# Conv FFNs on the unnormalised residual: inverse norm at the eviction, tap products from SBUF, norm weight inside the high/low split

## What is computed

```
def rms_norm_2(x, g):
    xf = x.astype(jnp.float32)
    y = xf * lax.rsqrt(jnp.mean(xf * xf, axis=-1, keepdims=True) + NORM_EPS)
    return (y * g.astype(jnp.float32)).astype(x.dtype)

def causal_dwconv(h, w, b):
    c = h.shape[-1]
    y = lax.conv_general_dilated(h, w[:, None, :].astype(h.dtype), (1,), [(CONV_WIDTH - 1, 0)],
                                 dimension_numbers=('NWC', 'WIO', 'NWC'), feature_group_count=c)
    return y + b

def conv_ffn(h, w_up, conv_w, conv_b, w_down):
    u = causal_dwconv(h @ w_up, conv_w, conv_b)
    gate, up = jnp.split(u, 2, axis=-1)
    return (jax.nn.silu(gate) * up) @ w_down
```

## Time and profile before

| | us |
|---|---|
| median of 3 runs | 1832.31 |
| lowest, highest | 1828.08, 1835.67 |
| span of the profiled execution | 1831.9 |
| conv_0, up phase (first to last matmul) | 1267.4 to 1397.0 |
| conv_1, up phase | 1624.8 to 1753.2 |
| PE busy in the span | 1700.7 (93%) |
| DVE busy | 1185.9 (65%) |
| ACT busy | 904.3 (49%) |

### The profile page before, as it was taken

How to read it: one execution, slowest core, us unless ns; L and a number is a source line. 1 busy time by engine, 2 the same in 40 slices (tenths; PEclk the granted TensorE clock), 3 DMA queues, 4 the chain that set the end, 5 groups by cost and what they waited for, 6 DMA issues and landing times.

```text
span 1831.9 us, 33959 instructions
## 1 busy us (share of the span) xinstructions
PE 1700.7 (93%) x13128; PEld 1636.6 (89%) x13128; DVE 1185.9 (65%) x1907; ACT 904.3 (49%) x1546; POOL 14.2 (1%) x20
## 2 busy tenths in 40 slices
PE   6999999899999999996899999878999989779997
PEld 5999997799999999975799999767999988679997
DVE  6555656576666666667666665767886576578764
ACT  5544453454445444454454454355665442356652
POOL 1000000000000000000000000000000000000000
PEclk9999999899999999998899999988999999989999
DMA  7554552255446554540255456204554543035442
GB/s 270 177 182 144 205 199 104 70 202 184 174 155 217 184 183 142 204 153 35 81 197 182 160 166 236 92 15 166 183 184 140 197 190 108 34 137 182 169 158 86
DMA packets 47358, 286.11 MB, mean 156 GB/s; under 512 B 5996, under 2 KB 6764, under 8 KB 23968
## 3 DMA queue, kind: packets, MB, share of 16 engines
q1 hardware_dynamic: 44640, 278.94, 43.5%
q10 hardware_dynamic: 2240, 5.19, 0.8%
q0 software_dynamic: 384, 0.68, 0.1%
HBM read 283.74 MB, written 1.05 MB: 155 GB/s over the span
## 4 chain that ended last, share of the span: by engine, by line
PE 84%; DVE 9%; ACT 4%; issue 2%; DMA 0%; ACTq 0%; DVEq 0%
PE ps_gemm L129 78%; DVE s_wlo L89 3%; ACT s_whi L80 1%; ACT s_work L839 1%; PE ps_gemm L828 1%; PE ps_sum L178 1%; PE ps_gemm L803 1%; DVE s_small L879 1%; DVE s_work L875 1%; PE ps_s L803 1%; PE ps_sum L828 1%; ACT s_work L848 1%; PE ps_sum L760 0%; DVE s_work L898 0%; PE ps_gemm L1161 0%
## 5 line engine op out<-in xcount | busy, mean ns | idle before, releaser
L89 DVE TENSOR_TENSOR s_wlo<-s_wraw,s_whi 128x1024 fp32r<-128x1024 f32 (+3 forms) x608 | 629.5, 1077 | 491.6 <-ACT s_whi L80 491.5
L80 ACT ACTIVATE s_whi<-s_wraw 128x1024 fp32r<-128x1024 f32 (+3 forms) x608 | 539.7, 935 | 445.3 <-PE ps_gemm L129 438.3
L129 PE MATMUL ps_gemm<-s_xhi,s_whi 128*128 128x256 f32 x2504 | 717.2, 286 | 13.4 <-DVE s_xlo L239 9.0
L129 PE MATMUL ps_gemm<-s_xlo,s_whi 128*128 128x256 f32 x2504 | 711.7, 284 | 0.0
L129 PE MATMUL ps_gemm<-s_xhi,s_wlo 128*128 128x256 f32 x2504 | 711.6, 284 | 0.0
L129 PEld LDWEIGHTS ps_gemm<-s_xhi,s_whi 128*128 128x128 f32 x2504 | 483.9, 193 | 18.1 <-issue 11.3
L129 PEld LDWEIGHTS ps_gemm<-s_xlo,s_whi 128*128 128x128 f32 x2504 | 484.0, 193 | 1.3 <-issue 1.0
L129 PEld LDWEIGHTS ps_gemm<-s_xhi,s_wlo 128*128 128x128 f32 x2504 | 483.9, 193 | 0.0
L129 PE MATMUL ps_gemm<-hid_hi,s_whi 128*128 128x256 f32 x1344 | 381.4, 284 | 12.4 <-DVE s_wlo L89 6.9
L129 PE MATMUL ps_gemm<-hid_hi,s_wlo 128*128 128x256 f32 x1344 | 381.3, 284 | 0.0
L129 PE MATMUL ps_gemm<-hid_lo,s_whi 128*128 128x256 f32 x1344 | 380.9, 283 | 0.0
(11 more groups left out here) (322 smaller groups left out, 1248.8 us busy)
## 6 DMA issues: line engine op xcount, KB each, us to landing
s_wraw<-in_stream_dram SPq DMA_DIRECT2D x178, 1024.0 KB, 4.8
s_wraw<-in_stream_dram SPq DMA_DIRECT2D x96, 704.0 KB, 4.1
s_wraw<-in_stream_dram SPq DMA_DIRECT2D x16, 768.0 KB, 4.3
s_wraw<-in_stream_dram SPq DMA_DIRECT2D x14, 512.0 KB, 3.3
...
```

The source lines that it names most:

```text
L80: c.act.activation(c.whi[:, slot, s], c.wraw[:, raw, s], ACT.Copy).then_inc(c.hi_ready, 1)
L89: last = c.dve.tensor_tensor(c.wlo[:, slot, s], c.wraw[:, raw, s], c.whi[:, slot, s].bitcast(F32), ALU.subtract)
L129: last = pe.matmul(out, a, b, start=start and i == 0, stop=stop and i == 2, skip_group_check=skip)
```

## The change

`conv_0` and `conv_1` join `LATE_SCALED`. The mixer's `post_norm` now makes the split ahead for them, and the sums of squares stand between the products of their first unit. In the up iteration VectorE scales the bank by the inverse norm into a new SBUF tile `c.scaled`, which frees the bank. ScalarE's tap 2 reads `c.scaled` and waits for it through `bank_free`; the four products read it too. The rest of the split of tile j-1 moves ahead of the products, and a new semaphore `linear_ready` tells the end of the last product.

In all stages that are scaled late, the separate multiplication by the norm weight goes (it stays for mix_a, which needs `c.xn2`): ScalarE's rounding carries the weight as its scale, and VectorE's subtraction becomes `x * weight - high` in one instruction.

```
-LATE_SCALED = ("mix_a", "ffn2_0", "ffn1_1", "mix_b", "ffn2_1", "mix_e", "mix_o")
+LATE_SCALED = ("mix_a", "ffn2_0", "ffn1_1", "mix_b", "ffn2_1", "mix_e", "conv_0", "mix_o", "conv_1")
+KEPT_SCALED = ("mix_a",)
...
-    c.act.wait_ge(c.xn_ready, cnt.xn + n + 1 + step)
-    c.act.activation(c.xhi2[:, s], c.xn2[:, s], ACT.Copy).then_inc(c.xhi_ready, 1)
+    c.act.activation(c.xhi2[:, s], c.x2[:, s], ACT.Identity, scale=ahead.column(c, n, turn)).then_inc(c.xhi_ready, 1)
...
+    g = ahead.column(c, n, turn)
+    if ahead.kept:
+        c.dve.tensor_scalar(c.xn2[:, s], c.x2[:, s], g, None, ALU.mult).then_inc(c.xn_ready, 1)
     c.dve.wait_ge(c.xhi_ready, cnt.xn + n + 1 + step)
-    c.dve.tensor_tensor(c.xlo2[:, s], c.xn2[:, s], c.xhi2[:, s].bitcast(F32), ALU.subtract).then_inc(c.xlo_ready, 1)
+    c.dve.scalar_tensor_tensor(c.xlo2[:, s], c.x2[:, s], g, c.xhi2[:, s].bitcast(F32), ALU.mult,
+                               ALU.subtract).then_inc(c.xlo_ready, 1)
...
-            last = first_products_pe(c, cnt, bank, u, (c.xlo_ready, cnt.xn + 1), late)
+            last = first_products_pe(c, cnt, bank, u, (c.xlo_ready, cnt.xn + 1), late, name.startswith("conv"))
...
-        if not late:
-            act.wait_ge(c.unit_done, u0 + j + 1 + step)
-            if NF * cnt.two + j >= 2:
-                act.wait_ge(c.hid_ready, NF * cnt.two + j - 1 + step)
-        for side in range(0 if late else 2):
-            act.activation(c.cv[:, j % 2, side, :], c.ps_gemm[:, (g0 + j) % 4, side * T:(side + 1) * T], ACT.Identity,
+        if conv is not None:
+            act.wait_ge(c.bank_free, g0 + j + 1 + step)
+            act.wait_ge(c.hid_ready, NF * cnt.two + j - 1 + step)
+        for side in range(0 if conv is None else 2):
+            act.activation(c.cv[:, j % 2, side, :], c.scaled[:, j % 2, side, :], ACT.Identity,
...
+        dve.wait_ge(c.unit_done, u0 + j + 1 + step)
+        dve.tensor_tensor((c.cv if conv is None else c.scaled)[:, j % 2, :, :], bank.rearrange("p (a b) -> p a b", b=T),
+                          c.inv[:, :].unsqueeze(1).to_broadcast([P, 2, T]), ALU.mult).then_inc(c.bank_free, 1)
+        if j:
+            rest(j - 1, turn)
+        if conv is None:
+            dve.wait_ge(c.bank_free, g0 + j + 1 + step)
+            return
+        dve.wait_ge(c.tap_ready, 2 * m + 2 + step * 2)
+        for back in (1, 2):
             for side in range(2):
                 v = c.cv[:, j % 2, side, back:T]
                 if back == 2:
                     dve.wait_ge(c.back_done, 2 * m + side + 1 + step * 2)
-                ins = dve.scalar_tensor_tensor(v, bank[:, side * T:(side + 1) * T - back],
+                ins = dve.scalar_tensor_tensor(v, c.scaled[:, j % 2, side, 0:T - back],
                                                tap(c, conv, j, side, 2 - back, turn), v, ALU.mult, ALU.add)
-                ins.then_inc(c.back_done if back == 1 else c.conv_ready if side == 0 else c.bank_free, 1)
-        if j:
-            rest(j - 1, turn)
-        dve.wait_ge(c.bank_free, g0 + j + 1 + step)
+                ins.then_inc(c.back_done if back == 1 else c.conv_ready if side == 0 else c.linear_ready, 1)
+        dve.wait_ge(c.linear_ready, m + 1 + step)
```

More of the change, by code:

```diff
@@ L274, in ffn_pe @@
     late = name in LATE_SCALED
-    if name != "ffn1_0" and not late:
-        for k in range(KD):
-            norm_sums_pe(c, cnt, k)
     def up(j, turn):
@@ L366, in silu @@
     def silu(j, step):
-        if late:
+        if conv is None:
             act.wait_ge(c.bank_free, g0 + j + 1 + step)
@@ L412, in ffn_act @@
         cnt.two += 1
-        cnt.conv += not late
+        cnt.conv += conv is not None
     logs_act(c)
@@ L428, in output @@
                        after[:, bass.ds(turn * (2 * T) + n * T, T)], ACT.Square).then_inc(c.sq_ready, 1)
-        if ahead:
-            ahead_hi_act(c, cnt, n, turn, step)
+        if ahead is not None:
+            ahead_hi_act(c, ahead, n, turn)
     with act.Fori(0, KD // 2 - 1) as lap:
@@ L444, in ffn_act, with ffn_dve @@
         split_below(split_hi, c, cnt, u0 + 2 * KD + 2)
-def ffn_dve(c, cnt, name, conv, src, gain, ahead):
+def ffn_dve(c, cnt, name, conv, ahead):
     dve, u0, g0 = c.dve, FIRST_UNIT[name], cnt.out
     late = name in LATE_SCALED
-    if not late and name != "ffn1_0":
-        normed_dve(c, cnt, src, gain)
     split_below(split_lo, c, cnt, u0 + 2)
@@ L485, in convolved @@
         bank = c.ps_gemm[:, (g0 + j) % 4, :]
-        if late:
-            dve.wait_ge(c.unit_done, u0 + j + 1 + step)
-            dve.tensor_tensor(c.cv[:, j % 2, :, :], bank.rearrange("p (a b) -> p a b", b=T),
-                              c.inv[:, :].unsqueeze(1).to_broadcast([P, 2, T]), ALU.mult).then_inc(c.bank_free, 1)
-        else:
-            dve.wait_ge(c.tap_ready, 2 * m + 2 + step * 2)
-        for back in () if late else (1, 2):
+        dve.wait_ge(c.unit_done, u0 + j + 1 + step)
[3 more added lines that the diff above has]
+            rest(j - 1, turn)
+        if conv is None:
+            dve.wait_ge(c.bank_free, g0 + j + 1 + step)
+            return
+        dve.wait_ge(c.tap_ready, 2 * m + 2 + step * 2)
+        for back in (1, 2):
             for side in range(2):
@@ L537, in output @@
         ins.then_inc(c.bank_free, 1)
-        if ahead is not None:
-            dve.wait_ge(c.bank_free, g0 + n + 1 + step)
-            ahead_dve(c, ahead, n, turn)
         add_squares(c, cnt, n, n == 0 and turn is None, step)
         if ahead is not None:
-            ahead_lo_dve(c, cnt, n, turn, step)
+            ahead_lo_dve(c, cnt, ahead, n, turn, step)
     output(0, None)
@@ L572, in add_squares, with all_squares_act @@
     ins.then_inc(c.sq_added, 1)
-def all_squares_act(c, cnt, src, written, value, step=1, ahead=False):
+def all_squares_act(c, cnt, src, written, value, step=1, ahead=None):
     for k in range(KD):
@@ L581, in all_squares_act @@
         c.act.activation(c.sq[:, k % 2, :], src[:, k, :], ACT.Square).then_inc(c.sq_ready, 1)
-        if ahead:
-            ahead_hi_act(c, cnt, k, None, 0)
+        if ahead is not None:
+            ahead_hi_act(c, ahead, k, None)
     cnt.sq += KD
-    if ahead:
+    if ahead is not None:
         cnt.xn += KD
@@ L605, in post_norm_dve @@
             c.dve.tensor_tensor(c.x[:, k - 1, :], c.x[:, k - 1, :], c.xn[:, k - 1, :], ALU.add).then_inc(c.post_added, 1)
[L606 to L608 removed]
         if ahead is not None and 1 < k <= KD + 1:
[L610 removed]
+            ahead_lo_dve(c, cnt, ahead, k - 2, None, 0)
     if ahead is not None:
@@ L615, in post_norm_dve, with post_norm_act @@
     cnt.sq += KD
[L618 removed]
+def post_norm_act(c, cnt, ahead=None):
     inverse_act(c, cnt)
@@ L1072, in project_dve @@
         for k in range(n, n + wide):
-            if ahead is not None:
-                c.dve.wait_ge(c.bank_free, cnt.out)
-                ahead_dve(c, ahead, k, None)
             add_squares(c, cnt, k, k == 0, 0)
             if ahead is not None:
-                ahead_lo_dve(c, cnt, k, None, 0)
+                ahead_lo_dve(c, cnt, ahead, k, None, 0)
     if not post:
@@ L2308, in build @@
         c.gate, c.hid = (c.work[:, i * 2 * T:(i + 1) * 2 * T].rearrange("p (a b) -> p a b", b=T) for i in range(2))
-        c.cv = c.work[:, 4 * T:8 * T].rearrange("p (s a b) -> p s a b", s=2, b=T)
+        c.cv, c.scaled = (c.work[:, i * T:(i + 4) * T].rearrange("p (s a b) -> p s a b", s=2, b=T) for i in (4, 8))
         c.ss, c.pt = c.work[:, 0:3 * 1024].rearrange("p (a b) -> p a b", b=1024), c.work[:, 3 * 1024:4 * 1024]
```

48 lines of the change are left out of this document (22 added, 26 removed).

## The result

Before: 1833.99 us, median of 4 runs (1828.08 to 1837.52). Changed: 1892.61 us, median of 4 (1885.97 to 1894.08). The ratio is 1.0315, with a 95% interval of 1.0292 to 1.0337. I had forecast 1872 and a range up to 1884: the sign and the mechanism were right, the sum and the range were too short. The medians lie 58.6 us apart; the profiled executions have spans of 1892.2 and 1831.9, 60.3 us apart, where my sum had 39.5.

What follows compares the result with a forecast made beforehand. TensorE was taken to bound the kernel, with VectorE's longer cycle overtaking it in the conv up phases. Conv stages +14.2 and +14.8, handovers +12.2, mix_o -1.7 made +39.5 on 1831.9: 1871.4, forecast 1872 us, range 1853 to 1884.

Steps and rivals of the forecast that it cites:

- VectorE's cycle in the counted loop: Conv up phase: one looped VectorE iteration takes 7.01 us against TensorE's 5.76, costing about 21 us per conv stage.
- the rest of down is as before: Conv down phase from unit 24 on: no change in time.
- the 1.7 us that mix_o was to win: Boundary conv_0 to mix_o: dropping the separate norm-weight multiplication (L260) shortens it by 1.7 us.
- the handovers: Up to down in each conv stage: 15.8 us from the up phase's end to unit 24 against 9.7, +6.1 twice.
- The stall: Conv up phase: VectorE stands still 1.6 us per cycle through ScalarE's two taps and one rounding, lifting its cycle above TensorE's.
- S4: Start of VectorE's low half in iteration 4, at 41.4 us from the first post-norm multiplication, after three straight cycles.
- S19: Start of VectorE's low half in iteration 19, at 146.6 us from the first post-norm multiplication, after fifteen looped cycles.
- Taps and products from SBUF: Conv up phase: two taps take 1.05 us, 0.05 over now; products gain nothing from SBUF, within 0.02 us each.
- The boundary: Into the conv stages: sums of squares between the first unit's products win 7.1 us in conv_0 and 6.5 in conv_1.
- S0: Start of VectorE's low half in iteration 0, at 15.35 us from the first post-norm multiplication.
- the shorter chain: Rival in the up phase: shorter looped handoffs and taps give a 6.5 us cycle, 1852 us in all; chance 12%.
- the clock falls: Rival: TensorE, idle 1.2 us in every 7, drops to 1.2 GHz; 2034 us at most; chance 4%.

Runs made afterwards that it cites:

- e1: Changed kernel with ScalarE rounding tile j-1 ahead of the two taps of tile j instead of behind them; 1864.85 us, ratio 1.0168.
- e4: Changed kernel with taps and products reading PSUM, conv inputs not normalised; scaling still done into a tile nobody reads; 1831.39 us, ratio 0.9997.
- e6: Changed kernel with the counted loops of ScalarE's and VectorE's conv up phase written out; 1876.31 us, ratio 1.0248.
- e11: e3 with matmuls nobody reads in TensorE's pauses, fewer than e8 at the boundaries, plus 6 ahead of unit 24; 1818.36 us, ratio 0.9933.
- e9: Kernel before the change with only the norm weight folded into the split; conv stages as they were; 1832.78 us, ratio 1.0005.
- e2: Changed kernel with VectorE's rest of tile j-1 moved back behind the four tap products of tile j; 1867.44 us, ratio 1.0195.
- e10: e3 with the scaling of each conv tile done a second time, into a tile nobody reads; 1840.16 us, ratio 1.0044.
- e5: Like e9 on the kernel before, but by a slip without the weight multiplication in VectorE's low part of the activations; 1831.69 us, ratio 1.0000.
- e3: Changed kernel's same operations, reordered on VectorE and ScalarE so taps and rounding lie beside VectorE's low half; 1827.40 us, ratio 0.9980.
- e8: e3 with matmuls nobody reads in TensorE's boundary pauses, 10 before the last norm's sum and 24 behind it; 1826.55 us, ratio 0.9974.

## Why the prediction was right in its mechanism and short in its sum

The step that failed is the size of VectorE's cycle in the counted loop: 7.01 us in my sum, 7.28 measured in the mean, 8.0 us in both stages together. My range had room for that, as it reached to a cycle of 7.3. What carried the time 8.6 us beyond its end are terms without such room: "the rest of down is as before", where the clock fell (3.5 us), the 1.7 us that mix_o was to win (2.2), the handovers (1.0), and the spread of the stages ahead of conv_0 (3.7), which I had at nothing.

**The stall (right).** The chain of my cycle is in the trace link by link: low half to gate 2.28 (as said), gate to scaling 0.34 (0.33), scaling 0.68 (0.68), handoff 0.18 (0.14), two taps 1.10 (1.05), rounding less its overlap, and handoff, 0.47 (0.48), rest to products 0.34 (0.33), products 1.66 (1.64), completion 0.12 (0.08): 7.17 against 7.01. The straight cycle is 6.81 against 6.75; my own terms, with 0.04 for both handoffs, give 6.80, so I had added that up wrongly. e1 to e4 show that it is the chain.

**The cycle in the loop (the mis-sized term, 8.0 us).** I had left out the end of a lap. One cycle in four is 7.61 and the one behind it 7.27, so a lap has a mean of 7.31, not 7.01. From S4 to S19, fifteen cycles with three turns, it is 109.2 and 109.1 us, 7.28 each, where I had 105.2. Some 0.16 us of the 0.27 missing are in every cycle, the rest at the turns. I had read the loop's cost as a longer handoff (0.14 for 0.04) from a kernel whose loops are covered by TensorE, and there neither the lap's end nor the rest of it can be seen. e6 measured the loop whole: 16 us in the kernel.

**Taps and products from SBUF (right).** Products 479 ns against 474 from PSUM, so no gain. A tap takes 597 ns against 551 from PSUM, 46 more; I had 50. The Trainium skill, "VectorE: DVE Perf Modes", section on the TRN2 errata, has the two engines in one table: for VectorE a smaller fixed cost from SBUF, which these rows again don't show, for ScalarE 224 against 172 cycles, 43 ns at its 1.2 GHz, with which the 46 ns agree.

**The boundary (right in mechanism, 2.3 us short in both together).** The first product of conv_0 comes 6.3 us behind the mixer's last, where I had said about 6. But behind the multiplication it stands at 2.7 us in conv_0 and 3.1 in conv_1, not at 2.4. And I had taken two tiles, 3.29 us, and six more at 1.14 from a place where the clock rose early. In the changed kernel, with 0.57 to 0.64 granted over the 8 us behind the multiplications, the first two take 3.5 and 3.8 us in the conv stages, in mix_o the first three 5.7, and the last two take 1.26 and 1.71 us everywhere, in e11 at a clock of 1.00 too, so those are not the clock's. S0 comes at 15.8 and 16.5 us instead of 15.35. The four cycles behind it, 5.83, 6.81, 6.81 and 7.02, add 0.4 in each stage. From the multiplication to S4 conv_0 took 42.2 us instead of 41.4, conv_1 42.9.

How far the clock varies from execution to execution, the old boundary shows: in the profile of the kernel before the granted clock was 0.50 again over the first products of conv_0, in e9, with the same conv stage, 1.00, and unit 1 starts 19.5 us behind the multiplication in the one and 16.4 in the other.

```profile
1267.00:1273.00 6.00, 5.62 (x26) 5.65 (x27) 5.05 (x14) 3.92 (x8) 0.00 (x0) 0.50 0.30 128
```

```profile
1272.00:1278.00 6.00, 6.00 (x50) 6.00 (x51) 4.67 (x13) 3.79 (x7) 0.00 (x0) 1.00 0.33 139
```

Against e9 conv_0 would have lost 3.1 us more than the table shows.

**Handover (right).** From S19 to unit 24 24.5 us against 24.0.

**The rest of down "as before" (wrong, 3.5 us).** Same 462 matmuls, 57.32 and 57.54 instead of 55.70. The windows around the start of unit 24 and behind it:

```profile
1433.00:1440.00 7.00, 4.26 (x22) 3.98 (x21) 3.93 (x6) 3.67 (x6) 0.00 (x0) 0.51 0.38 114
1436.00:1450.00 14.00, 13.91 (x102) 13.94 (x103) 6.33 (x10) 4.17 (x8) 0.00 (x0) 0.86 0.50 158
1450.00:1493.00 43.00, 43.00 (x361) 43.00 (x359) 20.75 (x30) 18.77 (x27) 0.00 (x0) 1.00 0.60 215
```

TensorE comes out of the pause at half its clock. In the changed kernel that pause is 2.7 and 2.9 us, in the kernel before 1.76. The profiles of e1, e2, e4, e6 and e10 have 2.5 to 2.9 us there as well, and from unit 24 on all twelve down phases took 56.9 to 58.1. With a pause of 1.7 to 2.1 us (before, e5, e9, e3, e8) it isn't certain: ten of fourteen took 55.7, four 57.2; e3 alone has both 55.7 in one profile, both 57.2 in another, and one of each in the third. e11, which fills the pause, has 55.7 twice, too few to show that the filling did it. So the handover that the change lengthened brought its own cost on the clock, and my sum had none for it.

**conv_0 to mix_o (wrong, 2.2 us).** The first product came 0.4 us sooner, not 0.7, since ScalarE gets to its first square only behind a high half of the weights. Then the clock rose later than in the execution before: the fourth sum of squares (L179) stands 8.1 us behind the multiplication and is the first at full speed; before, it was the third, at 6.2 (1472.04). Unit 1 started at 14.8 instead of 14.3. With the clock held (e11) the forecast 1.7 is there.

**Ahead of conv_0 (not predicted, 3.7 us).** No difference of code shows there: from 357 to 778 us the FFN stages begin and end within 0.3 us of each other, and the gap opens in the mixers behind. In eight further profiles (e1, e2, the three of e3, e4, e6, e10) with the same code up to that point the multiplication starts between 1255.5 and 1261.7; e9, with the old conv stages, has 1261.5. It is a spread from execution to execution, and the kernel before was profiled near its early end. The mixers' granted clock, 0.79 to 0.86 over 820 to 893 in these profiles, goes with it for the most part (0.84 before, 0.79 in the changed kernel); that it is the cause was not tried.

Together 8.0 (loop) + 2.3 (boundaries) + 1.0 (handover) + 3.5 (down) + 2.2 (mix_o) + 3.7 (ahead) are 20.7 us, which with 39.5 make 60.2 of the 60.3 measured. Of the rivals none came true: the shorter chain (1852) was on the wrong side, and "the clock falls" happened, but at the boundaries and behind the handover, not inside the up phase, where the granted clock stayed at 1.00 through waits of 1.2 us. The Trainium skill, "TensorE: Matmul & The Clock Gate", section on a second HAM failure mode, tells of a kernel whose clock swung between its levels from short idle times between groups of matmuls; by that rule it would have swung here too, and the trace does not agree.
